# Where the split weights begin in on-chip memory, in a two-layer hybrid decoder trunk

## The reference

```python
def swiglu(h, wg, wu, wd):
    return (jax.nn.silu(h @ wg) * (h @ wu)) @ wd
...
    for layer in range(DEPTH):
        h = rms_norm(x, ffn_norm[layer, 0])
        x = x + 0.5 * swiglu(h, ffn_w_gate[layer, 0], ffn_w_up[layer, 0], ffn_w_down[layer, 0])
        h = rms_norm(x, mix_norm[layer])
        ...
        if layer % 2 == 0:
            x = x + hybrid_mixer(h, positions, ...)
        else:
            x = x + pool_mixer(h, pool_w[i], pool_scale[i])
        h = rms_norm(x, ffn_norm[layer, 1])
        x = x + 0.5 * swiglu(h, ffn_w_gate[layer, 1], ffn_w_up[layer, 1], ffn_w_down[layer, 1])
```

## Time and profile before

| | |
|---|---|
| two runs | 1744.35 and 1746.21 us, median 1745.28 |
| span of the profiled execution | 1744.6 us, first instruction to last (its own whole time isn't listed apart) |
| TensorE busy | 1731.3 us, 99% of the span, 8052 matmuls |
| weight loads (PEld) | 1415.9 us, 81% |
| VectorE, ScalarE, GpSimd | 821.2 (47%), 576.3 (33%), 120.0 us (7%) |
| DMA engines | 163.93 MB, about a third of their time |
| granted TensorE clock | 1.000 |

### The profile page before, as it was taken

The page is one execution under the profiler, slowest core; times in us unless marked ns, Lnnn a source line. Parts: engine busy times, 40 slices in busy tenths (PEclk is TensorE's granted clock), DMA queues, the critical chain, the costliest instruction groups (busy, mean ns, idle before and its releaser), DMA issues.

```text
span 1744.6 us, 21647 instructions
## 1 busy us (share of the span) xinstructions
PE 1731.3 (99%) x8052; PEld 1415.9 (81%) x8052; DVE 821.2 (47%) x1014; ACT 576.3 (33%) x796; POOL 120.0 (7%) x115
## 2 busy tenths in 40 slices
PE   8999999999999999999999999999999999999999
PEld 6888888887876688888888888888888888888887
DVE  5544443337788554444433254444332654444323
ACT  5333333233337443333322233333222533333211
POOL 0500000112014210000001000000011000000000
PEclk9999999999999999999999999999999999999999
DMA  6333343353420033333333233333332233333331
GB/s 180 104 97 96 96 115 92 94 123 76 100 64 26 18 102 98 97 96 96 111 103 103 81 96 97 96 96 103 106 95 70 85 97 96 96 96 114 100 99 48
DMA packets 321904, 163.93 MB, mean 94 GB/s; under 512 B 15140, under 2 KB 320264, under 8 KB 321864
## 3 DMA queue, kind: packets, MB, share of 16 engines
q1 hardware_dynamic: 321288, 162.92, 32.6%
q10 hardware_dynamic: 576, 0.48, 0.1%
HBM read 160.89 MB, written 2.10 MB: 93 GB/s over the span
## 4 chain that ended last, share of the span: by engine, by line
PE 97%; DVE 1%; DMA 1%; ACT 0%; issue 0%; ACTq 0%; SPq 0%; POOL 0%; DVEq 0%
PE ps_s L546 21%; PE ps_s L547 21%; PE ps_s L548 21%; PE ps_y L546 9%; PE ps_y L547 9%; PE ps_y L548 9%; PE ps_s L855 1%; PE ps_y L884 1%; PE ps_aux L904 1%; DMA x_in<-in_x 0%; PE ps_stat L741 0%; PE ps_s L852 0%; DVE w_lo L1435 0%; PE ps_s L778 0%; DMA partner<-work 0%
## 5 line engine op out<-in xcount | busy, mean ns | idle before, releaser
L1435 DVE TENSOR_TENSOR w_lo<-raw,w_hi 128x1024 fp32r<-128x1024 f32 (+2 forms) x272 | 357.7, 1315 | 717.7 <-ACT w_hi L1073 717.4
L546 PE MATMUL ps_s<-xg_hi,w_hi 128*128 128x512 f32 x1568 | 614.6, 392 | 0.2 <-DVE w_lo L1435 0.2
L548 PE MATMUL ps_s<-xg_hi,w_lo 128*128 128x512 f32 x1568 | 610.9, 390 | 0.0
L547 PE MATMUL ps_s<-xg_lo,w_hi 128*128 128x512 f32 x1568 | 610.9, 390 | 0.0
L1073 ACT CAST w_hi<-raw 128x1024 fp32r<-128x1024 f32 (+2 forms) x274 | 306.9, 1120 | 568.5 <-PE ps_y L548 290.5
L546 PEld LDWEIGHTS ps_s<-xg_hi,w_hi 128*128 128x128 f32 x1568 | 294.6, 188 | 64.7 <-issue 1.7
L547 PEld LDWEIGHTS ps_s<-xg_lo,w_hi 128*128 128x128 f32 x1568 | 294.6, 188 | 61.7 <-issue 1.4
L548 PEld LDWEIGHTS ps_s<-xg_hi,w_lo 128*128 128x128 f32 x1568 | 294.5, 188 | 61.0
L546 PE MATMUL ps_y<-act_hi,w_hi 128*128 128x512 f32 x695 | 270.9, 390 | 0.0
L548 PE MATMUL ps_y<-act_hi,w_lo 128*128 128x512 f32 x695 | 270.7, 389 | 0.0
L547 PE MATMUL ps_y<-act_lo,w_hi 128*128 128x512 f32 x695 | 270.7, 389 | 0.0
(11 more groups left out here) (321 smaller groups left out, 942.3 us busy)
## 6 DMA issues: line engine op xcount, KB each, us to landing
raw<-in_ffn_w_gate SPq DMA_DIRECT2D x88, 512.0 KB, 3.9
raw<-in_ffn_w_up SPq DMA_DIRECT2D x88, 512.0 KB, 3.9
raw<-in_ffn_w_down SPq DMA_DIRECT2D x64, 704.0 KB, 4.5
raw<-in_hyb_w_in SPq DMA_DIRECT2D x18, 512.0 KB, 3.9
x_in<-in_x SPq DMA_DIRECT2D x8, 256.0 KB, 6.4
w_raw<-in_hyb_cmp_w SPq DMA_DIRECT2D x4, 512.0 KB, 6.3
raw<-in_hyb_w_in SPq DMA_DIRECT2D x8, 256.0 KB, 3.7
raw<-in_hyb_w_out SPq DMA_DIRECT2D x16, 128.0 KB, 2.9
```

Of the source, the lines that this page charges most:

```text
L546: mm(bank, hi, x_hi, start=first, stop=False, **kw)
L547: mm(bank, hi, x_lo, start=False, stop=False, **kw)
L548: return mm(bank, lo, x_hi, start=False, stop=last, **kw)
L1435: tt(w_lo[:, n % 2, 0:size], raw[:, n % 4, 0:size], f32(w_hi[:, n % 2, 0:size]), ALU.subtract).then_inc(lo_ready, 1)
```

## The change

Each slot of `w_hi` and `w_lo` becomes 128 float32 longer (12 x 512 bytes instead of 11 x 512), and the weights no longer begin at the slot's start but `begins(high, n)` float32 behind it. That number is one of sixteen for the units of the feed-forwards, by feed-forward, by stretch (up or down) and by part (high or low), and 0 for all other units. In bytes:

| | first | second | third | fourth feed-forward |
|---|---|---|---|---|
| up, high | 256 | 128 | 64 | 32 |
| up, low | 384 | 192 | 96 | 16 |
| down, high | 320 | 448 | 16 | 160 |
| down, low | 0 | 480 | 224 | 288 |

These are the distances modulo 512 bytes from the activations, one of the sixteen being 0. The third feed-forward's down row holds for the four pooling units too. `piece` gives the access pattern, and takes the place of the slice wherever split weights are written or read. The tensors behind `w_hi` and `w_lo` move up by 1024 and 2048 bytes, so that no remainder by 512 changes. No instruction is added, removed or moved on any engine, and no semaphore, wait or transfer changes: only addresses do.

```diff
+HI_UP, LO_UP = (64, 32, 16, 8), (96, 48, 24, 4)
+HI_DOWN, LO_DOWN = (80, 112, 4, 40), (0, 120, 56, 72)
+
+
+def begins(high, n):
+
+    for ffn in range(4):
+        if U_FFN[ffn] <= n < U_FFN[ffn] + 2 * KF:
+            return (HI_UP if high else LO_UP)[ffn]
+        if U_FFN[ffn] + 2 * KF <= n < (U_FFN[3] if ffn == 2 else U_FFN[ffn] + 2 * KF + 2 * KD):
+            return (HI_DOWN if high else LO_DOWN)[ffn]
+    return 0
...
-        w_hi = sb("w_hi", [P, 2, KH2 * P], F32R)
-        w_lo = sb("w_lo", [P, 2, KH2 * P], F32R)
+        w_hi = sb("w_hi", [P, 2, KH2 * P + P], F32R)
+        w_lo = sb("w_lo", [P, 2, KH2 * P + P], F32R)
...
+        def piece(w, n, first, end):
+
+            at = begins(w is w_hi, n)
+            return w[:, n % 2, at + first:at + end]
...
-                    last_mm = three(bank, w_hi[:, n % 2, k * P:(k + 1) * P], w_lo[:, n % 2, k * P:(k + 1) * P],
+                    last_mm = three(bank, piece(w_hi, n, k * P, (k + 1) * P), piece(w_lo, n, k * P, (k + 1) * P),
...
-                copy(w_hi[:, n % 2, 0:BLOCKS[n] * P], raw[:, n % 4, 0:BLOCKS[n] * P]).then_inc(hi_ready, 1)
+                copy(piece(w_hi, n, 0, BLOCKS[n] * P), raw[:, n % 4, 0:BLOCKS[n] * P]).then_inc(hi_ready, 1)
...
-                tt(w_lo[:, n % 2, 0:size], raw[:, n % 4, 0:size], f32(w_hi[:, n % 2, 0:size]),
+                tt(piece(w_lo, n, 0, size), raw[:, n % 4, 0:size], f32(piece(w_hi, n, 0, size)),
```

More of the change, by code:

```diff
@@ L565, in high_first @@
                 for k in tiles:
-                    hi = w_hi[:, n % 2, k * P:(k + 1) * P]
+                    hi = piece(w_hi, n, k * P, (k + 1) * P)
                     mm(bank, hi, tile_of(x_hi, k0 + k), start=first and k == tiles[0], stop=False)
@@ L570, in high_first @@
                 for k in tiles:
-                    mm(bank, w_lo[:, n % 2, k * P:(k + 1) * P], tile_of(x_hi, k0 + k), start=False, stop=False)
+                    mm(bank, piece(w_lo, n, k * P, (k + 1) * P), tile_of(x_hi, k0 + k), start=False, stop=False)
             def first_unit():
@@ L579, in first_unit @@
                             turn_x(q, (KD - 1,))
-                    hi, lo = (w[:, 0, k * P:(k + 1) * P] for w in (w_hi, w_lo))
+                    hi, lo = (piece(w, 0, k * P, (k + 1) * P) for w in (w_hi, w_lo))
                     pe.wait_ge(xg_hi_ready, place + 1)
@@ L634, in block_of @@
                 def block_of(m, k):
-                    return three(ps_s[:, 2 * m, :], w_hi[:, (n + m) % 2, k * P:(k + 1) * P],
-                                 w_lo[:, (n + m) % 2, k * P:(k + 1) * P], tile_of(xg_hi, k), tile_of(xg_lo, k), k == 0, k == KD - 1)
+                    return three(ps_s[:, 2 * m, :], piece(w_hi, n + m, k * P, (k + 1) * P),
+                                 piece(w_lo, n + m, k * P, (k + 1) * P), tile_of(xg_hi, k), tile_of(xg_lo, k), k == 0, k == KD - 1)
                 for k in range(KD // 2):
@@ L956, in from_conv @@
                 for k in range(4, KD):
-                    three(ps_s[:, 2 + d % 2, :], w_hi[:, n % 2, k * P:(k + 1) * P], w_lo[:, n % 2, k * P:(k + 1) * P],
+                    three(ps_s[:, 2 + d % 2, :], piece(w_hi, n, k * P, (k + 1) * P), piece(w_lo, n, k * P, (k + 1) * P),
                           tile_of(ob_hi, k - 4), tile_of(ob_lo, k - 4), k == 4, False)
@@ L962, in from_attention @@
                 for k in range(4):
-                    last_mm = three(ps_s[:, 2 + d % 2, :], w_hi[:, n % 2, k * P:(k + 1) * P],
-                                    w_lo[:, n % 2, k * P:(k + 1) * P],
+                    last_mm = three(ps_s[:, 2 + d % 2, :], piece(w_hi, n, k * P, (k + 1) * P),
+                                    piece(w_lo, n, k * P, (k + 1) * P),
                                     tile_of(o_hi, k), tile_of(o_lo, k), False, k == 3)
@@ L991, in last_down @@
                 for k in range(3, KH2):
-                    last_mm = three(ps_y[:, d % 2, :], w_hi[:, n % 2, k * P:(k + 1) * P], w_lo[:, n % 2, k * P:(k + 1) * P],
+                    last_mm = three(ps_y[:, d % 2, :], piece(w_hi, n, k * P, (k + 1) * P), piece(w_lo, n, k * P, (k + 1) * P),
                                     tile_of(act_hi, h * KH2 + k), tile_of(act_lo, h * KH2 + k), False, h == 1 and k == KH2 - 1)
@@ L999, in mix @@
                 token_hi, token_lo = (x[:, (2 * g + k) * T + b * P:(2 * g + k) * T + (b + 1) * P] for x in (xg_hi, xg_lo))
-                w_h, w_l = (w[:, n % 2, k * 2 * P:(k + 1) * 2 * P] for w in (w_hi, w_lo))
+                w_h, w_l = (piece(w, n, k * 2 * P, (k + 1) * 2 * P) for w in (w_hi, w_lo))
                 mm(bank, token_hi, w_h, start=k == 0, stop=False)
@@ L1998, in split_low @@
                 pool.wait_ge(hi_ready, n + 1)
-                tt(w_lo[:, n % 2, 0:KD * P], raw[:, n % 4, 0:KD * P], f32(w_hi[:, n % 2, 0:KD * P]),
+                tt(piece(w_lo, n, 0, KD * P), raw[:, n % 4, 0:KD * P], f32(piece(w_hi, n, 0, KD * P)),
                    ALU.subtract).then_inc(lo_ready, 1)
```

## The result

The changed kernel takes 1777.23 us (two runs, 1776.76 to 1777.70) against 1745.28: ratio 1.0182, 95% interval 1.0152 to 1.0212. It is slower by 32 us; whether by more than 2% these two runs leave open. The profiled execution took 1777.7 us with a span of 1775.7, 31.1 longer than before.

What follows compares the result with a forecast made beforehand. TensorE's matmul pace, 226.67 ns a step, was taken to bound the kernel. Three terms of 0 left the span at 1744.6 us, plus 0.7 for the median: 1745.3 us, range 1722 to 1782 (about 0.8).

Steps and rivals of the forecast that it cites:

- the likeliest case: Feed-forward matmuls keep their pace of 226.67 ns: 1745.3 us, with chance 0.55 for 1743 to 1748.
- rival B: In all eight stretches: differing distances within a block break the rhythm; mild 1750 to 1780 us (0.16), hard over 1780 (0.11).
- What bounds the kernel: TensorE, busy 99% of the span, sets the time by its matmul pace; each nanosecond of pace is worth 6.34 us.
- Terms 1 and 2: ScalarE's casts and VectorE's subtractions at new addresses, and longer slots with shifted tensors behind them: 0 us each.
- Term 3: Weight load meeting stream at 6336 feed-forward matmuls: distance does not matter, taken as 0, range -84 to +53 us.
- The low end of term 3: The fastest end of the range of Term 3, over 6336 feed-forward matmuls: -84 us.
- rival A: Feed-forward matmuls: distance 0 is worst, others are faster; in part 1710 to 1742 us (0.08), mostly under 1710 (0.10).
- Rows 7 and 8: Trace rows from 645.34 and 1354.96 us: steps of 230 to 240 ns, read as following an interruption whatever the address.
- Rival C: Feed-forwards: only distance modulo 32 or 64 bytes matters, shifting at most 10 to 20 us; no chance of its own.

## Why the prediction was right or wrong

The measured 1777.2 lies in the range of 1722 to 1782 and within 2%, but the likeliest case, pace unchanged at 1745.3, didn't happen. What happened is the mild form of rival B, which had a chance of 0.16. That the range holds the time is owed to the room left for the rivals; the argument for the likeliest case was wrong.

- **What bounds the kernel.** Right. TensorE's pace is the time: 32 us by the paces, 31.1 by the spans, and no wait grew.
- **Terms 1 and 2, the writes and the shifted tensors, at 0.** Right: the four means moved by 4 ns at most, and with starts 8 bytes off a multiple of 16 they don't grow either (1225 and 1051 ns for a unit of 8 blocks, against 1230 and 1051). Moving everything by 96 bytes gave 0.9996.
- **Term 3, the meeting of load and stream, taken as 0.** This is the step that failed. It measured 31.1 us / 6336 = 4.9 ns a matmul. That the distance between load and stream wouldn't matter was my estimate, and it is refuted: the activations moved by 64 bytes alone gave 228.9, everything moved together gave 226.7. The same loads beside the same streams cost 226.7 or 234.3 ns a matmul, at a granted clock of 1.00, by nothing but the distance of their addresses. How load and stream fall into step over many matmuls seems to decide: costs don't add up load by load, and one pair has had paces of 231.1 and 233.3.
- **The low end of term 3, -84 us.** No run shows it, and the chance given to rival A leans on it. It would take a mean pace of 213.3 ns, and the lowest steady pace of any stretch is 226.67. What the rows hold is an estimate: at distance 0, 512 columns take 226.67 ns and 256 take 120, so that 256 more cost 106.7; in proportion, 13.3 ns of either don't go with the columns. That share isn't fixed: reckoned so, it is 6.7 ns for 256 columns with the loaded tile 64 bytes from the stream (113.3 ns), and up to 21 for 512 columns (234.3 at distance 96).
- **Rows 7 and 8.** I took 96's three steps of 230 ns, and the nine at 231 behind them, for the effect of an interruption. This reading was wrong, and the trace of before held the sign of what was to come: with the same two loads at distance 0 all twelve steps are at 226.7. Only the earlier trace rows, behind matmuls of another width, shows slow steps without a foreign distance. Distance 96 for good costs 234.3, more than those steps showed.
- **Rival A** (0 is the worst) had the sign wrong for the matmuls of 512 columns: of 23 distances tried none is under 226.7. For the 96 of 256 columns it had a point, 113.3 against 120 ns.
- **Rival B** had sign and near size: 3.3 ns and 1766 us for its mild form, 4.9 ns and 1777 measured. Its mechanism, two distances within a block, is only half of it: with one distance for both parts the time is the same 1777.1. The foreign distance suffices.
- **Rival C**, a smaller modulus, came true as 256 rather than 32 or 64, and then changes nothing here: only the high weights of the first up stretch are at 256, and 256 / 384 has the same 231.2 as 0 / 384.

What stays open: what it is, in the memory or in TensorE, that makes the distance count, why 0 and 240 are good while 244 and 248 are not, why 252 and 320 / 0 have two paces each, and why another distance is best at 256 columns. That the distance between loaded weights and stream makes the loss is shown; how it does so is not.

## What to carry to other kernels

Where a kernel is bound by matmuls with a weight load each, subtract starts in a long stretch: if fp32r matmuls of 512 columns start more than the 226.67 ns of this kernel apart at a granted clock of 1.00, the addresses may be part of it. For this shape let the weights begin at the same remainder modulo 256 bytes as the moving operand, as happens by itself when all tensors between the two are multiples of 256 bytes; distance 96 in all feed-forwards cost 2.7% here, and small tensors slipped in between activations and weights 0.8%. Other shapes have to be tried, since with 256 columns a distance of 64 was better than 0 (113.3 against 120 ns). A kernel of several long stretches can carry one candidate in each, so that one run measures eight.

## What the runs showed of the hardware

- With a new 128-column fp32r weight tile for each matmul of 512 fp32r columns at clock 1.00, the steady pace was 226.67 ns at distance 0 or 256 and 228.9 to 234.3 at most others; 240 was as good as 0, and 252 in one stretch of two.
- No stretch of 512 columns had a steady pace under 226.67 ns. With 256 columns it was 120 ns at distance 0 and 113.3 with the loaded tile 64 bytes on from the stream.
- Two loads at distance 96 in a stretch at distance 0 made twelve steps slow, 47 ns in all; with the same two at distance 0 there was none.
- The steady paces are not a continuum: 226.67, 228.9, 231.1 and 233.3 return again and again, in a block of three matmuls 680, 686.7, 693.3 and 700 ns, 6.7 ns apart; but 230.0, 230.7, 231.7, 231.8, 232.0, 232.4 and 234.3 exist too.
- At 320 / 0 the pace was 231.1 behind 256 / 384 (in two kernels) and 233.3 behind 256 / 0 (in two kernels as well). It outlives the units' boundaries within a stretch, and a slow pace ends when the distance is 0 again: 226.7 in the down stretches behind slow up stretches.
